# Output and down projections of a decoder layer with tokens on the output partitions

## What is computed

```python
x = x + merged @ w_out                                  # 1024 x 1024
f = rmsnorm(x, norm2_w) @ w_up                          # 1024 x 4096
x = x + jnp.square(jax.nn.relu(f)) @ w_down             # 4096 x 1024
y = rmsnorm(x, norm_f_w)
```

## Time and profile before

| | |
|---|---|
| median of 3 runs | 1697.22 us (1696.64 to 1697.35) |
| the profiled execution | 1696.56 us, its span 1694.8 us |
| granted TensorE clock, mean | 0.999 |
| busy share of the span | TensorE 99%, VectorE 43%, ScalarE 29%, GpSimd 26% |
| out projection | about 803.7 to 909.7 us |
| up and down, four groups | 909.7 to 1682.6 us |
| tail | 1682.6 to 1694.8 us |

### The profile page before, as it was taken

How to read it: one execution, slowest core, us unless ns; L and a number is a source line. 1 busy time by engine, 2 the same in 40 slices (tenths; PEclk the granted TensorE clock), 3 DMA queues, 4 the chain that set the end, 5 groups by cost and what they waited for, 6 DMA issues and landing times.

```text
span 1694.8 us, 28701 instructions
## 1 busy us (share of the span) xinstructions
PE 1674.5 (99%) x10876; PEld 1627.0 (96%) x10876; DVE 721.9 (43%) x1119; ACT 498.7 (29%) x939; POOL 432.4 (26%) x322
## 2 busy tenths in 40 slices
PE   9999999999999999999999999999999999999997
PEld 7999999999988888999999999999999999999997
DVE  6685977859612222365444331133211331123213
ACT  6555555546422222422333220022000220022102
POOL 4212212122121211232232323232323232232320
PEclk9999999999999999999999999999999999999999
DMA  5201112011185677442222111111111111111112
GB/s 157 64 26 52 51 38 66 26 53 42 59 278 175 200 234 233 164 147 66 78 77 76 38 50 38 50 38 50 40 47 46 41 50 37 50 38 50 38 50 106
DMA packets 171761, 136.17 MB, mean 80 GB/s; under 512 B 7935, under 2 KB 148379, under 8 KB 171676
## 3 DMA queue, kind: packets, MB, share of 16 engines
q1 hardware_dynamic: 171532, 134.96, 25.6%
q10 hardware_dynamic: 144, 0.04, 0.0%
HBM read 115.99 MB, written 18.98 MB: 80 GB/s over the span
## 4 chain that ended last, share of the span: by engine, by line
PE 84%; DVE 11%; ACT 3%; issue 2%; DMA 0%; SPq 0%; ACTq 0%; DVEq 0%
PE ps L962 75%; DVE sp L1722 3%; PE ps L1154 2%; DVE zc L1724 2%; DVE tl L1732 1%; DVE zc L1714 1%; PE ps L1198 1%; PE ps L1166 1%; ACT sp L1451 1%; PE ps L1110 1%; PE ps L1120 1%; PE ps L1137 1%; DVE br L1674 1%; PE ps L1136 1%; DVE zc L1715 1%
## 5 line engine op out<-in xcount | busy, mean ns | idle before, releaser
L875 POOL CAST wh<-raw 128x1024 fp32r<-128x1024 f32 x120 | 127.2, 1060 | 1066.2 <-issue 494.6
L884 POOL TENSOR_TENSOR wl<-raw,wh 128x1024 fp32r<-128x1024 f32 x120 | 291.3, 2428 | 150.5 <-DVE zc L1724 119.2
L962 PE MATMUL ps<-xh,wh 128*128 128x364 f32 (+1 forms) x956 | 323.7, 339 | 2.5 <-DVE xl L1699 1.1
L962 PE MATMUL ps<-xl,wh 128*128 128x364 f32 (+1 forms) x956 | 313.8, 328 | 0.0
L962 PE MATMUL ps<-xh,wl 128*128 128x364 f32 (+1 forms) x956 | 313.8, 328 | 0.0
L962 PE MATMUL ps<-yh,wh 128*128 128x364 f32 (+1 forms) x768 | 253.0, 329 | 0.0
L962 PE MATMUL ps<-hh,wh 128*128 128x364 f32 (+1 forms) x768 | 252.7, 329 | 0.0
L962 PE MATMUL ps<-yl,wh 128*128 128x364 f32 (+1 forms) x768 | 252.4, 329 | 0.0
L962 PE MATMUL ps<-hl,wh 128*128 128x364 f32 (+1 forms) x768 | 252.4, 329 | 0.0
L962 PE MATMUL ps<-yh,wl 128*128 128x364 f32 (+1 forms) x768 | 252.3, 329 | 0.0
L962 PE MATMUL ps<-hh,wl 128*128 128x364 f32 (+1 forms) x768 | 252.3, 329 | 0.0
(11 more groups left out here) (172 smaller groups left out, 2455.7 us busy)
## 6 DMA issues: line engine op xcount, KB each, us to landing
raw<-in_w_in SPq DMA_DIRECT2D x80, 256.0 KB, 3.6
cache<-in_cache_k SPq DMA_DIRECT2D x64, 256.0 KB, 3.6
cache<-in_cache_v SPq DMA_DIRECT2D x64, 256.0 KB, 3.6
raw<-in_w_up SPq DMA_DIRECT2D x64, 256.0 KB, 3.0
raw<-in_w_down SPq DMA_DIRECT2D x64, 256.0 KB, 3.0
gates<-gst SPq DMA_DIRECT2D x16, 544.0 KB, 6.0
gb<-gates SPq DMA_DIRECT2D x16, 544.0 KB, 5.6
raw<-in_w_out SPq DMA_DIRECT2D x16, 256.0 KB, 3.7
```

Of the source, the lines that this page charges most:

```text
L875: g.tensor_copy(wh[s][:, :], raw[s][:, :]).then_inc(w_hi, 1)
L884: g.tensor_tensor(wl[s][:, :], raw[s][:, :], f32(wh[s][:, :]), ALU.subtract).then_inc(w_split, 1)
L962: ins = mm(out, lhs[:, k * P:(k + 1) * P], rhs[:, x], start=(first and a == 0 and m == 0), stop=(last and a == n - 1 and m == 2))
```

## The change

The out and down projections turn their roles around: 128 tokens are the stationary operand, 512 output columns of a weight row block move, and the result has tokens on the partitions (`by_rows`). The six PSUM banks hold six such results (token block b, column half h) at once, so that the projection goes in passes over token blocks (`PASSES`): in out three blocks and both halves at a time; in the first three down groups blocks 0 to 5 with one half each, then blocks 6 to 8 with both. Weight tiles are one row block with 1024 columns, or two row blocks with 512, and each pass loads and splits its own. In the last down group the first pass (blocks 0 to 2) keeps its eight split tiles (`big_h`, `big_l`), and blocks 3, 4, 5, 8, 6, 7 follow one by one, each half a chain of its own.

`x1` now lies as rows and is loaded as it stands in memory; the turns of the input fall away. Each block is normalised as a row (square with sum, root, reciprocal, scaled copy), turned once (`turn_y`, 8 transposes into banks 6 and 7) and split into `yh` and `yl` in 8 parts of 128 columns on ScalarE, then on VectorE. The relu step of up has no factor any more, and the three sums over partitions go. Up keeps its form with chunks of 384, 384 and 320 tokens. For the 64 sample tokens the low half of `mh` and `hh` lies in 64 more columns beside the high half, so that one stationary operand has both, and the two halves of the result are added later (`low_rows`). At the end no block is turned; the last one is finished in halves. One list, `tail`, gives the order on all engines.

```diff
+        T3 = [(0, 3 * P), (3 * P, 6 * P), (6 * P, NTOK)]
+        PASSES = {-1: [((0, 1, 2), (0, 1)), ((3, 4, 5), (0, 1)), ((6, 7, 8), (0, 1))],
+                  NQ - 1: [((0, 1, 2), (0, 1))]}
+        for g in range(NQ - 1):
+            PASSES[g] = [(tuple(range(6)), (0,)), (tuple(range(6)), (1,)), ((6, 7, 8), (0, 1))]
...
+        tail = []
+        for p in range(3):
+            beside_tile = {0: [("norm", 3 * p - 3)], 1: [("norm", 3 * p - 2)], 2: [("turn_y", 3 * p - 3), ("norm", 3 * p - 1)],
+                           4: [("turn_y", 3 * p - 2)], 6: [("turn_y", 3 * p - 1)]}
+            for q in range(KT):
+                tail.append(("rows", -1, p, q))
+                if p:
+                    tail.extend(beside_tile.get(q, ()))
+        tail += [("norm", 6), ("norm", 7), ("norm", 8)]
+        tail += [("up", 0, 0, 0), ("turn_y", 6), ("up", 0, 0, 1), ("turn_y", 7), ("up", 0, 1, 0), ("turn_y", 8), ("up", 0, 1, 1),
+                 ("up", 0, 0, 2), ("up", 0, 1, 2)]
+        for g in range(NQ):
+            tail += [("up", g, j, c) for j in range(2 if g == 0 else 0, KT) for c in range(3)]
+            for p in range(len(PASSES[g])):
+                tail += [("rows", g, p, q) for q in range(KT // deep(g, p))]
+        tail.insert(len(tail) - 2, ("wf_spread",))
+        tail += [("final", b) for b in PASSES[NQ - 1][0][0]]
+        for b in LAST_BLOCKS:
+            if b != LAST_BLOCKS[-1]:
+                tail += [("block", b, 0), ("block", b, 1), ("final", b)]
+            else:
+                tail += [("block", b, 0), ("final_half", b, 0), ("block", b, 1), ("final_half", b, 1)]
...
+            for n in range(len(TILES)):
+                if n < 2:
+                    used = (proj_done, 3 * KT - 3 + 3 * n)
+                elif n < BIG_FROM:
+                    used = (step_done, tile_end[TILES[n - 2]])
+                else:
+                    used = (step_done, LAST_UP)
+                high, low = by_hand(n)
+                split(T1 + n // 2, n % 2, used, high)
+                split_lo(n % 2, 2 * T1 + n, None, high, low)
...
+            def by_rows(g, b, h, k, w, lo_w):
+
+                t = step_no[g, b, h]
...
+                high, low = (mh, ml) if g < 0 else (hh, hl)
+                out, last = step_bank(t), k == KT - 1
+                hi = high[:, k * HW + b * P:k * HW + b * P + P]
+                if b < NB:
+                    lo = low[:, k * SEQ + b * P:k * SEQ + b * P + P]
+                    mm(out, hi, w, start=k == 0, stop=False)
+                    mm(out, lo, w, start=False, stop=False)
+                    return mm(out, hi, lo_w, start=False, stop=last)
+
+                mm(out, hi, w, start=k == 0, stop=False)
+                return mm(out, hi, lo_w, start=False, stop=last)
...
+                if e[0] == "rows":
+                    _, g, p, q = e
+                    n = tile_no[e]
+                    pe.wait_ge(w_split, base + n + 1)
+                    if g < 0:
+                        if p == 0:
...
+                        elif q == 0:
+                            pe.wait_ge(m_lo, 3 * KT)
+                    elif q == 0:
+                        pe.wait_ge(h_lo, h_no[g, KT - 1, 2 if PASSES[g][p][0][-1] == NB else 1] + 1)
...
+                    high, low = by_hand(n)
+                    for kk in range(deep(g, p)):
+                        k = q * deep(g, p) + kk
+                        for b, h in itertools.product(*PASSES[g][p]):
+                            at = (h if deep(g, p) == 1 else kk) * 512
+                            ins = by_rows(g, b, h, k, high[:, at:at + 512], low[:, at:at + 512])
+                            if k == KT - 1:
+                                ins.then_inc(step_done, 1)
+                    if k < KT - 1:
+                        ins.then_inc(step_done, 1)
...
+                elif e[0] == "block":
+                    _, b, h = e
+                    if (b, h) == (LAST_BLOCKS[0], 0):
+                        pe.wait_ge(h_lo, len(h_no))
+                    for k in range(KT):
+                        high, low = by_hand(tile_no["rows", NQ - 1, 0, k])
+                        ins = by_rows(NQ - 1, b, h, k, high[:, h * 512:h * 512 + 512], low[:, h * 512:h * 512 + 512])
+                    ins.then_inc(step_done, 1)
...
+                    pe.wait_ge(n_scaled, b + 1)
+                    if b:
+                        pe.wait_ge(y_lo, b)
                     for f in range(KT):
...
+                        ins = tr(ps[:, 6 * 512 + f * P:6 * 512 + f * P + n], x[0:n, f * P:f * P + P], ident[0:n, 0:n])
+                    ins.then_inc(n_turned, 1)
+                elif e[0] == "up":
+                    _, g, j, c = e
+                    n, t, (a, z) = tile_no[e[:3]], step_no[e], T3[c]
+                    pe.wait_ge(w_split, base + n + 1)
+                    pe.wait_ge(step_free, t + 1)
+                    if g == 0:
+                        pe.wait_ge(y_lo, 3 * c + 3)
+                    product(step_bank(t, 0, z - a), wh[n % 2], wl[n % 2], range(KT), yh, yl, (a, z)).then_inc(step_done, 1)
...
+            for e in tail:
+                if e[0] == "norm":
...
+                    act.wait_ge(step_free, step_no[-1, b, 1] + 1 + 6)
+                    if b == NB:
+                        A(x[0:SMP, :], x1[SMP:P, b * D:(b + 1) * D], ACT.Copy).then_inc(low_moved, 1)
+                        act.wait_ge(low_added, 1)
+                    A(x[0:n, :], own, ACT.Square, accum_out=r[0:n, 0:1]).then_inc(n_squared, 1)
+                    act.wait_ge(n_squared, b + 1)
+                    A(r[0:n, 1:2], r[0:n, 0:1], ACT.Sqrt, scale=1.0 / D, bias=eps[0:n, 0:1]).then_inc(n_root, 1)
+                    act.wait_ge(n_rec, b + 1)
+                    A(x[0:n, :], own, ACT.Copy, scale=r[0:n, 2:3]).then_inc(n_scaled, 1)
+                elif e[0] == "turn_y":
+                    b = e[1]
+                    n = rows_in(b)
+                    act.wait_ge(n_turned, b + 1)
+                    for f in range(KT):
+                        ins = A(yh[:, f * NTOK + b * P:f * NTOK + b * P + n], ps[:, 6 * 512 + f * P:6 * 512 + f * P + n], ACT.Copy,
+                                scale=w2c[:, f:f + 1])
+                    ins.then_inc(y_hi, 1)
+                elif e[0] == "up":
+                    _, g, j, c = e
+                    (a, z), m = T3[c], h_no[e[1:]]
+                    act.wait_ge(step_free, step_no[e] + 1 + 6)
+                    A(ts_[m % 2][:, 0:z - a], tt[m % 2][:, 0:z - a], ACT.Square).then_inc(s_made, 1)
+                    act.wait_ge(s_made, m + 1)
+                    A(hh[:, j * HW + a:j * HW + z], ts_[m % 2][:, 0:z - a], ACT.Copy).then_inc(h_hi, 1)
...
+            def add_rows(g, b, h):
+
...
+                    v.wait_ge(x1_in[p], 16 * 3)
+                if b == NB:
+                    v.wait_ge(low_zeroed, 1 if g < 0 else 2)
+                v.wait_ge(step_done, done_no[g, b, h])
+                x = x1[:, part(b, h)]
+                V_.tensor_tensor(x, step_bank(step_no[g, b, h]), x, ALU.add).then_inc(step_free, 1)
+
+            def h_low(g, j, c):
...
+                v.wait_ge(h_hi, m + 1)
+                ins = V_.tensor_tensor(hl[:, j * SEQ + a:j * SEQ + e], ts_[m % 2][:, 0:e - a], f32(hh[:, j * HW + a:j * HW + e]), ALU.subtract)
...
+            late_low = []
+            for e in tail:
+                if e[0] != "up" and late_low:
+                    h_low(*late_low.pop())
+                if e[0] == "rows":
+                    _, g, p, q = e
+                    if q == KT // deep(g, p) - 1:
+                        for b, h in itertools.product(*PASSES[g][p]):
+                            add_rows(g, b, h)
...
+                elif e[0] == "norm":
+                    b = e[1]
+                    n, r = rows_in(b), stat[b]
+                    if b == NB:
+                        v.wait_ge(step_free, step_no[-1, b, 1] + 1 + 6)
+                        add_low(b, xn[b - 4][0:SMP, :], 1)
+                        V_.memset(x1[SMP:P, NB * D:], 0.0).then_inc(low_zeroed, 1)
+                    v.wait_ge(n_root, b + 1)
+                    V_.reciprocal(r[0:n, 2:3], r[0:n, 1:2]).then_inc(n_rec, 1)
+                elif e[0] == "turn_y":
+                    b = e[1]
...
+                    v.wait_ge(y_hi, b + 1)
+                    for f in range(KT):
+                        x = slice(f * NTOK + b * P, f * NTOK + b * P + n)
+                        ins = V_.scalar_tensor_tensor(out=yl[:, x], in0=ps[:, 6 * 512 + f * P:6 * 512 + f * P + n], scalar=w2c[:, f:f + 1],
+                                                      in1=f32(yh[:, x]), op0=ALU.mult, op1=ALU.subtract)
...
+                elif e[0] == "up":
+                    _, g, j, c = e
+                    (a, z), m, t = T3[c], h_no[e[1:]], step_no[e]
+                    v.wait_ge(step_done, done_no[e])
+                    V_.tensor_scalar(tt[m % 2][:, 0:z - a], step_bank(t, 0, z - a), 0.0, None, ALU.max).then_inc(step_free, 1)
```

(59 more changed lines are left out.)

422 lines of the change are left out of this document (180 added, 242 removed).

## The result

| | before | after |
|---|---|---|
| median of 6 runs each, same chip | 1697.12 us (1696.64 to 1697.35) | 1704.05 us (1703.21 to 1705.25) |
| ratio, 95% interval | | 1.0042 (1.0029 to 1.0055) |
| profiled execution, its span | 1696.56, 1694.8 us | 1705.25, 1703.5 us |
| mean granted TensorE clock | 0.999 | 0.996 |

The account below looks back on a forecast made before the run. TensorE, busy for 99% of the span, was taken to bound the kernel. From the out projection on, the terms summed to 900.3 us for 891.1, +9.2, so 1706.5 us for the median, range 1697 to 1715.

Parts of the forecast that it names:

- Products: Out and down projections: 2080 products of 512 columns at 0.230 us take 478.4 us against 479.2, so nothing is gained.
- the first rival: Out and down products have a fixed price: 512 columns take 216 ns, 29 us go, 1677 us; chance 6%.
- Up: Up projection with chunks of 384, 384, 320: 495 ns for 499, 768 times, 380.2 us for 383.4.
- Turns: Nine groups of transposes turning the normalised blocks cost 7.6 us; block 2's turn makes the next pass 0.9 us late.
- Norm: Start of up: TensorE waits 10.6 us for blocks 6 to 8, of which 7.9 before block 7's turn.
- The timetable: Engine steps from the out projection's end: six adds until 4.4 us, block 7's turn due at 10.9, held 7.9.
- Clock: After the hole before block 7's turn, 4 to 5 us of work run at 1.2 GHz: +2.4 us (0 to 4).
- Up to down: Down's first tile waits for the last up tile's second-chunk low half: four times 1.85, 7.4 us.
- Weights: Last passes of out and down: each second weight tile about 0.44 us late, 5.8 us in all, 5.3 in down.
- Tail: End of the run, last block finished in halves: 7.0 us after the last product, for 12.2 before.
- hidden waits: Rival: only 2 to 6 of the 13 us at up's start stay, low half not held; 1690 to 1700, chance 14%.
- supply: Rival: weight supply bounds the three-block passes too, up to 13 us more, 1712 to 1720; chance 10%.

Follow-up runs that it names:

- the last run of all: Changed kernel with waits taken out, 384, 384, 320 chunks in the first stage, low parts awaited later, order set by hand, no extra transposes: 1674.40 us, ratio 0.9867.

## Why the prediction was right, and where it was not

The sign, the size and most of the mechanisms stood: the savings at the two ends, and waits at the seams that outweigh them. The sum is 2.4 us above the median, and 1.4 above the trace that the terms below are read from (900.3 for 898.9). That it is so near is in part luck: terms that were 8.9 us too high, the products first, met 7.5 us that were too low or not forecast.

- **Products.** Forecast 478.4, measured 2080 x 0.227 = 472.2. The step that failed is the spacing of 0.230, read from one pair of rows to 0.01 us: 3 ns too much, times 2080. It was the largest miss, 6.2 us. "Hardly a fixed part" is wrong too: pairs read to 0.01 us (230, 160 to 170 and 166) can't show 13 ns. The rule of the Trainium skill in "TensorE: Matmul & The Clock Gate", section "Wait — 56ns, not 53.3ns?", has a fixed part too, but 2.5 ns and 215.7 ns at 512 columns; the traces have about 13 and 227, so the measurement decides, and the first rival (1677) did not come.
- **Up.** 380.2 forecast; 768 x 0.493 = 378.6. (The forecast's 174 + 174 + 147 for its chunks are not 0.45 ns a column, as it says, which would be 490, but a little over 0.455.)
- **Turns.** 7.4 for 7.6, 109 ns each. Block 2's turn held the next pass for 1.2 us (0.9).
- **Norm.** Waits 1.6, 8.6 and 1.0 (forecast 1.6, 7.9, 1.1). Only the second is what the forecast describes. The 1.6 was forecast in front of block 6's turn, behind its reciprocal; it came in front of up's first product, which had to wait for the first of the six adds. The timetable has these adds at the right time, but not that up needs the bank that they free; that the two waits are equally long is luck. And 0.7 of the 1.0 is a weight tile: the product at 947.71 waited for GpSimd's difference (L974), since the order at the start of up keeps the first tile's buffer in use until its third chunk, and GpSimd's cast of the next tile began only at 943.9. Clock: about 3.0 of TensorE's work, of which keeping the clock up gave back 2.4 in the traces (2.4 forecast).
- **Up to down.** 4 x 1.87 = 7.5 (7.4); confirmed by taking it alone, 7.8.
- **Weights.** 8.2 in the last passes of down for 5.3, and 0.5 in out as forecast. The short gaps are 0.46 each (0.35 and 0.11) as the path of 4.03 had it. What was missing is a late load in each pass. In the changed kernel a packet of 16 KB from the queue that brings instructions lies on that load (1099.0 us: 1.8 us long); in the run with extra transposes in the hole two of the three passes have no such packet beside the loads of their own tiles and no long gap, and the third has both; with the norms reordered a packet of 1.2 us (1295.2) went with a gap of only 0.3; in the last run of all, packets of 0.9 and 1.0 went with no long gap, one of 1.9 with the gap of 1.3. No experiment moved the packets alone, so this is a coincidence in time and not a cause shown.
- **Not forecast:** 0.9 us in the first pass of out (821.9), where the loads of the input rows lie beside a weight load; taken out together with others only.
- **Tail.** 7.0 forecast, from TensorE's last slot (1697.4) to the end (1703.5) 6.1.

The terms as measured give 896.8 us, the trace 898.9; the other 2.1 us are excesses of some ns at bank and tile changes that I can't assign. Of the rivals, hidden waits fell with the 8.6 us hole, and supply was right in kind, with 3 of its 13 us.

The stages after the waits are gone (1674.40) tell what the new form is worth: down groups 94.7, 94.5, 96.1 against 94.9 for the old form in chunks of 384, so nothing to speak of; the out projection 99.9 against 105.0 and the last projection with its tail 100.5 against 111.6, since nothing is turned; up group 0 101.2 against 96.7, still its price. Against the old form so cut (1685.10) it is 10.7 us faster, and it came out ahead only once its waits were repaired one by one. Of the 7.0 us that the products of out and down gained, the new cut of the old form alone would have given 4.4 (960 triples at 494.6 ns are 474.8 us, an estimate); turning the roles gave 2.6.

## What to carry to other kernels

Where TensorE is busy for 99% of the time, a restructured projection is judged by the waits it makes at its seams: make a timetable of each in-order queue there, and where one list orders several engines, check the steps of each by itself. Of two buffers, compare the path from release to ready with one tile's time, not the helper's load, and let the first consumer ask only for the part that it reads first. In such a timetable put down when each PSUM bank is freed, too: here a wait came in front of a product for which the forecast had none. Before you restructure for wider instructions, measure the spacing of other cuts of the present form: here 384, 384 and 320 columns for 364, 364 and 360, as many instructions and columns, gave 11.6 us.

## What the runs showed of the hardware

- fp32r products start 120 ns apart at 256 columns, 147 at 320, 173 at 384 and 227 at 512: about 13 ns and 0.418 ns a column. Those of 364 and 360 columns start 166.4 apart, 1.8 above this line. Products of 256 columns, each with a weight load of 188 ns, ran at 120 ns.
- After a hole of 8.6 us the granted clock was low (0.50 from 926 to 930), which cost 2.4 us of the run; with the norms reordered it was low for a while after a hole of 2.4 us (mean 0.81 from 917 to 926) and again after one of 3.8 (0.52 from 930 to 936); holes of 1.2 and 1.9 us left it at 1.00.
- VectorE's difference for a chunk of 364 or 360 columns (L1857 of the kernel before) took 0.52 to 0.53 us alone, 1.10 to 1.12 where it began beside GpSimd's cast of a weight tile, and 2.26 to 2.27 beside GpSimd's own difference.
